# Two units side by side between the chunks of x, and own buffers for the third unit

## Chip, cores, metric

One core of one Trainium2 chip. The metric is the device time of one execution in microseconds (us).

## What is computed

One decoder layer over 16 learned tokens and 512 prompt positions, and for 8 decode sequences with a cache: 536 tokens in all, 1024 channels, in this order:

```python
x = x + 0.5 * (silu(h @ w_gate1) * (h @ w_up1)) @ w_down1     # h = rmsnorm(x)
u, q, k, v = project(rmsnorm(x))                              # QK-norm, partial rotary
x = x + concat(pool_mix(u), window_attention(q, k, v)) @ w_out
x = x + 0.5 * (silu(h @ w_gate2) * (h @ w_up2)) @ w_down2     # h = rmsnorm(x)
```

The inner width of both feed-forward halves is 2816, that is 22 blocks of 128. All of it is float32.

## The kernel before

Everything lies transposed: channels on the 128 partitions, tokens along the rows. x is 8 chunks (`xT[:, k, :]`, 128 channels x 536 tokens, 268 KB). Each operand of a large product is split in two: a high part, rounded to the type that TensorE takes in one pass (`xhi`, `whi`), and the rest (`xlo`, `wlo`). A product is then three: high by high, weights' high by x's low, weights' low by x's high. ScalarE makes the high parts, VectorE the low ones, and semaphores count what is done. A matmul takes 268 tokens, so each of the three comes as two matmuls.

The first half of the layer begins with "plain" units, the change's place. A unit is one block of 128 columns of gate or up weights: 8 tiles of 128x128, 512 KB, 48 matmuls. Units 0 and 1 are gate and up of the first block, 2 and 3 of the second, and so on up to unit 7; unit c is loaded into `raw[:, c % 3]` and split into `whi[:, c % 2]` and `wlo[:, c % 2]` (`whi_of`, `wlo_of`, lines 420 to 424). Behind them, from line 740 on, stand larger blocks that use a scheme with fewer products; their weights' high parts are in `whi7`.

The order on each engine is written out by hand:

- SyncE (lines 521 to 531) loads the first two tiles of unit 0 (`FIRST`), two chunks of x, the other six tiles, six chunks of x, then units 1 and up. x comes in `ORDER` 0, 2, 4, 6, 1, 3, 5, 7. A load into a slot of `raw` that is taken again waits for the low part that was made from it (line 477).
- ScalarE (lines 1306 to 1330) makes the high parts in that order, then the split of unit 1, the squares of x (`sqx`) with the split of unit 2 behind the fourth, the even chunks scaled (`x_even`), a table load for the root, the split of unit 3, the root of the norm, and the first sums of the later scheme (`t_hi`). From unit 2 on a split waits for the unit before the last one, whose buffer it takes (line 1117).
- VectorE (lines 1765 to 1797) makes the low parts, scales two small tables, makes the low part of unit 1, adds the squares up one after the other with the low part of unit 2 behind the fourth sum, then four terms of `t_sums`, the low part of unit 3, and the reciprocal of the root (`invert`).
- TensorE (lines 693 to 708) runs `WARM` products of zeros, then `early`: unit 0's high parts chunk by chunk, its products with x's low parts, unit 1 in the same manner. Unit 2 stands in three pieces with the norm between them:

```python
plain(2, turn, [0, 1])
norm_sums(0, 0, n)          # waits for all seven sums of squares
plain(2, turn, [2, 3])
norm_spread(0, 0, n, 1)     # waits for the reciprocal
plain(2, turn, [4, 5, 6, 7])
```

Then come unit 3 (it waits for the spread norm) and units 4 to 7.

Of the kernel before, what the change touches and what calls it, by code (L numbers as in the profile page):

```python
# [39 lines left out]
P = 128  # L40
# [69 lines left out]

NORM_AT = (1, 2, 6)
SQSUM_AT = (0, KD - 1, 2 * (KD - 1))
WARM = 6
FIRST = 2
ORDER = (0, 2, 4, 6, 1, 3, 5, 7)


# [31 lines left out]
def build(nc, a):  # L149
# [90 lines left out]
    dq, o = place("dq", [P, NDEC, KVH, GQ], offset=o)  # L240
    assert o <= h_at

    o = whi7_at
    ckT, o = place("ckT", [P, NDEC, P], offset=o)
    cv, o = place("cv", [P, NDEC, P], offset=o)
# [46 lines left out]
    def sem(name):  # L292
        return ctx.enter_context(nc.semaphore(name))
# [1 line left out]
    x_loaded = [sem(f"x_loaded{k}") for k in range(KD)]  # L295
    fixed_loaded = sem("fixed_loaded")
    gains_loaded = sem("gains_loaded")
    first_loaded = sem("first_loaded")
    first_hi = sem("first_hi")
    first_lo = sem("first_lo")  # L300
    mixin_loaded = sem("mixin_loaded")
# [116 lines left out]
              dict(s=1, ua=U_A2, ub=U_B2, ea=E_A2, eb=E_B2, c0=META, n=NH_OUT)]  # L418

    def whi_of(c):  # L420
        return whi3 if c == U_OUT + 2 else whi[:, c % 2, :, :]

    def wlo_of(c):
        return wlo3 if c == U_OUT + 2 else wlo[:, c % 2, :, :]

    def blocks(n):

# [45 lines left out]
    def _(sp):  # L473
# [40 lines left out]
        def downs(s, p):  # L514

            for d in range(KD):
                load_down(s, p, d)
                if d == 3 and p < 2:
                    load_unit(s, p + 1, 0)

        sp.dma_start(raw[:, 0, 0:FIRST, :].rearrange("p t c -> p (t c)"), a["gu1"][:, 0:FIRST * P]
                     ).then_inc(first_loaded, 16)
        for k in ORDER:
            sp.dma_start(xT[:, k, :], a["x"][:, k, :]).then_inc(x_loaded[k], 16)
            if k == ORDER[FIRST - 1]:
                sp.dma_start(raw[:, 0, FIRST:KD, :].rearrange("p t c -> p (t c)"), a["gu1"][:, FIRST * P:KD * P]
                             ).then_inc(raw_loaded[0], 16)
        for u in range(1, 2 * PLAIN[0]):
            load_plain(0, u)
            if u == 5:  # L530
                load_unit(0, 0, 0)
# [68 lines left out]
    def _(pe):  # L600
# [31 lines left out]
            for _ in range(WARM):  # L632
                nc.tensor.matmul(nsum[:, 0, 0:2 * P], hid[:, 0:P], hid[:, 0:2 * P], start=True, stop=True)

        def early(c, dst, pairs, n, wait, first=False, last=False):

            x = x_split(n)
            for t, k in enumerate(ORDER):
                for i, (w, lo) in enumerate(pairs):
                    wait(t, i)  # L640
                    for h in range(2):
                        done = nc.tensor.matmul(dst[:, h, 0:n], w[:, c % 2, t, :], x(k, lo, h),  # L642
                                                start=(first and t == 0 and i == 0),
                                                stop=(last and t == KD - 1 and i == len(pairs) - 1))
            if last:
                done.then_inc(unit_done, 1)

        def norm_sums(i, c0, n):

# [17 lines left out]
        def plain_products_1():  # L667

            n = NH_ALL

            def hi_there(t, i):
                if i == 0:
                    pe.wait_ge(xhi_ready, t + 1)
                if t == 0:
                    pe.wait_ge(first_lo if i else first_hi, 1)
                elif t == FIRST:
                    pe.wait_ge(wlo_ready if i else whi_ready, 1)

            def lo_there(t, i):
                pe.wait_ge(xlo_ready, t + 1)  # L680

            def hi_1(t, i):
                if t + i == 0:
                    pe.wait_ge(whi_ready, 2)

            def lo_1(t, i):
                if t == 0:
                    pe.wait_ge(wlo_ready, 2)

            def plain(c, dst, ks=None):  # L690
                product(c, dst, KD, x_split(n), n, None, ks, chunk)

            warm_up()
            early(0, pair[0], [(whi, 0), (wlo, 0)], n, hi_there, first=True)
            early(0, pair[0], [(whi, 1)], n, lo_there, last=True)
            early(1, pair[1], [(whi, 0), (whi, 1)], n, hi_1, first=True)
            early(1, pair[1], [(wlo, 0)], n, lo_1, last=True)
            plain(2, turn, [0, 1])
            norm_sums(0, 0, n)
            plain(2, turn, [2, 3])  # L700
            norm_spread(0, 0, n, 1)
            plain(2, turn, [4, 5, 6, 7])
            pe.wait_ge(rstd_ready, 1)
            plain(3, nsum)
            for f in (2, 3):
                for j in range(2):
                    pe.wait_ge(evacuated, E_A1 + 2 * f + j - (3 if f == 2 else 1))
                    plain(2 * f + j, pair[j])
# [391 lines left out]
    def _(act):  # L1100
# [7 lines left out]
        def split_hi(c):  # L1108

            t = tiles_of(c)  # L1110
            act.wait_ge(raw_loaded[c % RAW], 16 * (c // RAW + 1))
            if c == U_OUT + 2:
                act.wait_ge(sin_ready, 5)
                act.wait_ge(rot_ready, 5)
                act.wait_ge(nsum_filled, 5)
            elif c >= 2:
                act.wait_ge(unit_done, c - 1)
            nc.scalar.copy(whi_of(c)[:, 0:t, :], raw[:, c % RAW, 0:t, :]).then_inc(whi_ready, 1)  # L1118

# [185 lines left out]

        act.wait_ge(consts_made, 2)
        nc.scalar.copy(warm[:, :], eps[:, :]).then_inc(warmed, 1)
        act.wait_ge(first_loaded, 16)
        nc.scalar.copy(whi[:, 0, 0:FIRST, :], raw[:, 0, 0:FIRST, :]).then_inc(first_hi, 1)
        act.wait_ge(gains_loaded, 16)  # L1310
        for k in ORDER:
            act.wait_ge(x_loaded[k], 16)
            x_hi(x_pair(xhi7, k, NH_ALL), k, 0, 0, NH_ALL)
            if k == ORDER[FIRST - 1]:
                act.wait_ge(raw_loaded[0], 16)
                nc.scalar.copy(whi[:, 0, FIRST:KD, :], raw[:, 0, FIRST:KD, :]).then_inc(whi_ready, 1)
        split_hi(1)
        for k in range(KD):
            nc.scalar.activation(sqx[:, k, :], xT[:, k, :], ACT.Square).then_inc(sqx_ready, 1)
            if k == 3:  # L1320
                split_hi(2)
        late_consts()
        for pr in range(KC):
# [178 lines left out]
    def _(dve):  # L1502
# [259 lines left out]
                    if d:  # L1762
                        add_square(1, d, 0, NH_ALL)

        def first_weights_lo(hi_there, tiles):

            dve.wait_ge(hi_there, 1)
            return nc.vector.tensor_tensor(wlo[:, 0, tiles, :], raw[:, 0, tiles, :], whi[:, 0, tiles, :].bitcast(F32),
                                           ALU.subtract)

        first_weights_lo(first_hi, slice(0, FIRST)).then_inc(first_lo, 1)
        dve.wait_ge(gains_loaded, 16)
        for t, k in enumerate(ORDER):
            x_lo(x_pair(xlo7, k, NH_ALL), x_pair(xhi7, k, NH_ALL), t, k, 0, 0, NH_ALL)
            if t == FIRST - 1:
                first_weights_lo(whi_ready, slice(FIRST, KD)).then_inc(wlo_ready, 1)
        dve.wait_ge(fixed_loaded, 16)
        nc.vector.tensor_scalar(nsink[:, :], fixed[:, C_SINK:C_IDENT], -1.0, None, ALU.mult)
        nc.vector.tensor_scalar(ngain[:, :], gains[:, 0:3 * KD], -1.0, None, ALU.mult).then_inc(ngain_made, 1)
        split_lo(1)  # L1780

        for k in range(1, KD):
            dve.wait_ge(sqx_ready, k + 1)
            if k > 1:
                dve.wait_ge(sqx_summed, k - 1)
            nc.vector.tensor_tensor(sqx[:, 0, :], sqx[:, 0, :], sqx[:, k, :], ALU.add).then_inc(sqx_summed, 1)
            if k == 4:
                split_lo(2)
        dve.wait_ge(ngain_made, 1)
        n = NH_ALL  # L1790
# [434 lines left out]
```

## Time and profile before

| | us |
|---|---|
| median of the runs | 882.77 (881.46 to 883.40, 3 runs) |
| profiled execution, its time | 880.45 |
| profiled execution, its span | 878.4 |
| TensorE busy in the span | 871.3 (99%) |
| VectorE, ScalarE, GpSimd busy | 660.3, 394.0, 32.4 |

Times in the rows are from the start of the span. A row names line, engine, operation, what is written and read, and a count; matmuls overlap, so that the length of a group is from the first start to the last end.

### The profile page before, as it was taken

The numbers are of one execution on the slowest core, as the hardware profiler recorded it, in microseconds if no ns is written. First come the engines' busy times: TensorE is split into PE (matmuls) and PEld (weight loads), VectorE is DVE, ScalarE is ACT, GpSimd is POOL, SyncE is SP. The second block draws the span as 40 slices with busy tenths as digits, with TensorE's granted clock in tenths as the row PEclk, the third lists the DMA queues.
The fourth block names the chain that finished last, engine by engine and source line by source line (L and its number), as shares of the span: only waits on it lengthen the run. The fifth ranks groups of instructions, "written<-read, shape, count | busy, mean of one in ns | idle before, by whom it ended". The sixth has DMA issues, their size and how long they took to land.

```text
span 878.4 us, 17072 instructions
## 1 busy us (share of the span) xinstructions
PE 871.3 (99%) x7088; PEld 856.9 (98%) x7088; DVE 660.3 (75%) x979; ACT 394.0 (45%) x639; POOL 32.4 (4%) x37
## 2 busy tenths in 40 slices
PE   8999999999999999999999999999999999999998
PEld 7999999999999999999888999999999999999998
DVE  6979647997569986754887697996479975799754
ACT  7635313554224553443754465554125542255420
POOL 0000000000000000012423000000000000000000
PEclk9999999999999999999999999999999999999999
DMA  7333323332424322522321415324233324334241
GB/s 251 117 121 114 133 66 121 121 121 84 145 65 164 121 76 84 190 76 60 113 65 60 145 38 169 120 76 175 75 121 120 121 85 145 111 122 128 85 121 61
DMA packets 43180, 98.57 MB, mean 112 GB/s; under 512 B 4288, under 2 KB 5056, under 8 KB 43104
## 3 DMA queue, kind: packets, MB, share of 16 engines
q1 hardware_dynamic: 41376, 95.01, 33.6%
q10 hardware_dynamic: 1728, 2.48, 0.8%
q8 instruction: 56, 0.92, 0.4%
q14 instruction: 20, 0.16, 0.1%
HBM read 93.53 MB, written 3.60 MB: 111 GB/s over the span
## 4 chain that ended last, share of the span: by engine, by line
PE 96%; DVE 2%; DMA 1%; issue 1%; ACT 0%; SPq 0%; DVEq 0%; ACTq 0%
PE ps L612 44%; PE ps L740 15%; PE ps L742 15%; PE ps L741 15%; PE ps L642 1%; PE ps L978 1%; PE ps L969 1%; DMA xT<-x 1%; PE ps L960 1%; PE ps L799 1%; PE ps L933 0%; PE ps L883 0%; PE ps L657 0%; DVE wlo L1522 0%; DVE hlo L1649 0%
## 5 line engine op out<-in xcount | busy, mean ns | idle before, releaser
L740 PE MATMUL ps<-xhi,whi 128*128 128x260 f32 (+1 forms) x1092 | 310.2, 284 | 0.1
L742 PE MATMUL ps<-xhi,wlo 128*128 128x260 f32 (+1 forms) x1092 | 310.0, 284 | 0.0
L741 PE MATMUL ps<-xlo,whi 128*128 128x260 f32 (+1 forms) x1092 | 309.6, 284 | 0.0
L740 PEld LDWEIGHTS ps<-xhi,whi 128*128 128x128 f32 x1092 | 205.4, 188 | 0.8 <-issue 0.6
L742 PEld LDWEIGHTS ps<-xhi,wlo 128*128 128x128 f32 x1092 | 205.5, 188 | 0.0
L741 PEld LDWEIGHTS ps<-xlo,whi 128*128 128x128 f32 x1092 | 205.4, 188 | 0.0
L1593 DVE TENSOR_TENSOR wlo<-full,whi 128x1024 fp32r<-128x1024 f32 (+1 forms) x117 | 160.3, 1394 | 0.0
L1118 ACT CAST whi<-raw 128x1024 fp32r<-128x1024 f32 (+1 forms) x75 | 75.2, 1003 | 154.9 <-PE ps L612 147.9
L612 PE MATMUL ps<-hhi,whi 128*128 128x268 f32 (+1 forms) x690 | 140.4, 285 | 0.3
L612 PE MATMUL ps<-hlo,whi 128*128 128x268 f32 (+1 forms) x690 | 140.1, 284 | 0.0
L612 PE MATMUL ps<-hhi,wlo 128*128 128x268 f32 (+1 forms) x690 | 139.8, 284 | 0.0
L612 PEld LDWEIGHTS ps<-hhi,whi 128*128 128x128 f32 x690 | 106.8, 188 | 1.1 <-DVE hlo L1649 1.1
L612 PEld LDWEIGHTS ps<-hhi,wlo 128*128 128x128 f32 x690 | 107.0, 188 | 0.0
L612 PEld LDWEIGHTS ps<-hlo,whi 128*128 128x128 f32 x690 | 106.7, 188 | 0.0
L1522 DVE TENSOR_TENSOR wlo<-raw,whi 128x1024 fp32r<-128x1024 f32 (+1 forms) x75 | 90.2, 1204 | 16.9 <-ACT whi L1118 16.8
L1689 DVE SCALAR_TENSOR_TENSOR gate<-ps,rstd 128x536 f32<-128x536 f32 (+1 forms) x47 | 33.2, 707 | 81.6 <-PE ps L612 81.2
L1178 ACT CAST whi<-full 128x1024 fp32r<-128x1024 f32 x39 | 41.1, 1053 | 106.4 <-issue 89.6
L612 PE MATMUL ps<-xhi,whi 128*128 128x268 f32 (+1 forms) x288 | 60.5, 291 | 0.0
L612 PE MATMUL ps<-xhi,wlo 128*128 128x268 f32 (+1 forms) x288 | 58.7, 285 | 0.0
L612 PE MATMUL ps<-xlo,whi 128*128 128x268 f32 (+1 forms) x288 | 58.5, 285 | 0.0
L1192 ACT CAST whi<-full 128x1536 fp32r<-128x1536 f32 x39 | 57.8, 1483 | 0.0
L1578 DVE TENSOR_TENSOR full<-full 128x1024 f32<-128x1024 f32 x39 | 47.4, 1216 | 0.0
(194 smaller groups left out, 1070.4 us busy)
## 6 DMA issues: line engine op xcount, KB each, us to landing
full<-gu SPq DMA_DIRECT2D x78, 512.0 KB, 4.4
raw<-d SPq DMA_DIRECT2D x32, 448.0 KB, 3.5
full<-gu SPq DMA_DIRECT2D x39, 256.0 KB, 2.7
raw<-d SPq DMA_DIRECT2D x16, 512.0 KB, 3.7
raw<-w_in SPq DMA_DIRECT2D x10, 512.0 KB, 3.7
raw<-gu SPq DMA_DIRECT2D x9, 512.0 KB, 4.3
raw<-w_out SPq DMA_DIRECT2D x8, 512.0 KB, 4.3
xT<-x SPq DMA_DIRECT2D x8, 268.0 KB, 5.8
```

Source lines behind the costliest of these rows:

```text
L612: last = nc.tensor.matmul(dst[:, h, 0:n], w[:, kk, :], x(k, lo, h), start=(k == begin and i == 0), stop=(k == end and i == 2))
L642: done = nc.tensor.matmul(dst[:, h, 0:n], w[:, c % 2, t, :], x(k, lo, h), start=(first and t == 0 and i == 0), stop=(last and t == KD - 1 ...
L740: nc.tensor.matmul(dst, whi_t, xhi_t, start=(first and pr == 0), stop=False, skip_group_check=True)
L741: nc.tensor.matmul(dst, whi_t, xlo_t, start=False, stop=False, skip_group_check=True)
L742: last = nc.tensor.matmul(dst, wlo_t, xhi_t, start=False, stop=(pr == KC - 1), skip_group_check=True)
L1118: nc.scalar.copy(whi_of(c)[:, 0:t, :], raw[:, c % RAW, 0:t, :]).then_inc(whi_ready, 1)
L1178: nc.scalar.copy(whi7[:, i % 2, 0:2, :], full[:, i % 3, 0:2, :]).then_inc(hi_ready[0], 1)
L1192: nc.scalar.copy(whi7[:, i % 2, 4:7, :], full[:, i % 3, 4:7, :]).then_inc(hi_ready[2], 1)
L1522: nc.vector.tensor_tensor(wlo_of(c)[:, 0:t, :], raw[:, c % RAW, 0:t, :], whi_of(c)[:, 0:t, :].bitcast(F32), ALU.subtract).then_inc(wlo_rea ...
L1578: nc.vector.tensor_tensor(full[:, r, 1:5:3, :], full[:, r, 1:5:3, :], full[:, r, 0:7:6, :], ALU.add).then_inc(added, 1)
L1593: nc.vector.tensor_tensor(wlo7[:, i % 3, b, :], full[:, i % 3, b, :], whi7[:, i % 2, b, :].bitcast(F32), ALU.subtract).then_inc(lo_ready[g ...
L1689: nc.vector.scalar_tensor_tensor(out=halves(gate[:, cols], n), in0=pair[d % 2][:, :, 0:n], scalar=-0.5, in1=halves(rstd[:, cols], n), op0= ...
```

## The change

The loads of units 0 and 1 are cut into three pieces each (two, two and four tiles) and stand between the chunks of x: ahead of the first chunk unit 0's first piece, ahead of the second unit 1's first, ahead of the third both second pieces, ahead of the fifth both last ones. ScalarE and VectorE split each piece in the same place of their order. TensorE takes the two units side by side: for each chunk of x the products with its high part for both units, then those with the low part of the chunk before. Both units end together. One warm-up product is dropped. The split of unit 2 goes to buffers of its own (`whi_u2`, `wlo_u2`, in the second half of `whi7`, which is free until the later scheme's second block), doesn't wait for unit 0, and moves from behind the fourth square to behind the second; its low part moves from behind the fourth sum to behind the first.

```diff
--- before.py
+++ after.py
@@ -110,8 +110,10 @@
 
 NORM_AT = (1, 2, 6)
 SQSUM_AT = (0, KD - 1, 2 * (KD - 1))
-WARM = 6
-FIRST = 2
+WARM = 5
+PIECES = ((0, 2), (2, 4), (4, 8))
+
+BEFORE_X = {0: ((0, 0),), 1: ((1, 0),), 2: ((0, 1), (1, 1)), 4: ((0, 2), (1, 2))}
 ORDER = (0, 2, 4, 6, 1, 3, 5, 7)
 
 
@@ -240,6 +242,9 @@
     dq, o = place("dq", [P, NDEC, KVH, GQ], offset=o)
     assert o <= h_at
 
+    whi_u2, o = place("whi_u2", [P, KD, P], F32R, offset=whi7_at + 7 * BLK * 4)
+    wlo_u2, o = place("wlo_u2", [P, KD, P], F32R, offset=o)
+    assert o <= w_end
     o = whi7_at
     ckT, o = place("ckT", [P, NDEC, P], offset=o)
     cv, o = place("cv", [P, NDEC, P], offset=o)
@@ -295,7 +300,7 @@
     x_loaded = [sem(f"x_loaded{k}") for k in range(KD)]
     fixed_loaded = sem("fixed_loaded")
     gains_loaded = sem("gains_loaded")
-    first_loaded = sem("first_loaded")
+    piece_loaded = [[sem(f"piece_loaded{c}{j}") for j in range(2)] for c in range(2)]
     first_hi = sem("first_hi")
     first_lo = sem("first_lo")
     mixin_loaded = sem("mixin_loaded")
@@ -418,10 +423,10 @@
               dict(s=1, ua=U_A2, ub=U_B2, ea=E_A2, eb=E_B2, c0=META, n=NH_OUT)]
 
     def whi_of(c):
-        return whi3 if c == U_OUT + 2 else whi[:, c % 2, :, :]
+        return {2: whi_u2, U_OUT + 2: whi3}.get(c, whi[:, c % 2, :, :])
 
     def wlo_of(c):
-        return wlo3 if c == U_OUT + 2 else wlo[:, c % 2, :, :]
+        return {2: wlo_u2, U_OUT + 2: wlo3}.get(c, wlo[:, c % 2, :, :])
 
     def blocks(n):
 
@@ -518,14 +523,16 @@
                 if d == 3 and p < 2:
                     load_unit(s, p + 1, 0)
 
-        sp.dma_start(raw[:, 0, 0:FIRST, :].rearrange("p t c -> p (t c)"), a["gu1"][:, 0:FIRST * P]
-                     ).then_inc(first_loaded, 16)
-        for k in ORDER:
+        def load_piece(c, j):
+            lo, hi = PIECES[j]
+            sp.dma_start(raw[:, c, lo:hi, :].rearrange("p t c -> p (t c)"), a["gu1"][:, (c * KD + lo) * P:(c * KD + hi) * P]
+                         ).then_inc(raw_loaded[c] if j == 2 else piece_loaded[c][j], 16)
+
+        for t, k in enumerate(ORDER):
+            for c, j in BEFORE_X.get(t, ()):
+                load_piece(c, j)
             sp.dma_start(xT[:, k, :], a["x"][:, k, :]).then_inc(x_loaded[k], 16)
-            if k == ORDER[FIRST - 1]:
-                sp.dma_start(raw[:, 0, FIRST:KD, :].rearrange("p t c -> p (t c)"), a["gu1"][:, FIRST * P:KD * P]
-                             ).then_inc(raw_loaded[0], 16)
-        for u in range(1, 2 * PLAIN[0]):
+        for u in range(2, 2 * PLAIN[0]):
             load_plain(0, u)
             if u == 5:
                 load_unit(0, 0, 0)
@@ -632,18 +639,31 @@
             for _ in range(WARM):
                 nc.tensor.matmul(nsum[:, 0, 0:2 * P], hid[:, 0:P], hid[:, 0:2 * P], start=True, stop=True)
 
-        def early(c, dst, pairs, n, wait, first=False, last=False):
+        def first_two(n):
 
             x = x_split(n)
-            for t, k in enumerate(ORDER):
-                for i, (w, lo) in enumerate(pairs):
-                    wait(t, i)
-                    for h in range(2):
-                        done = nc.tensor.matmul(dst[:, h, 0:n], w[:, c % 2, t, :], x(k, lo, h),
-                                                start=(first and t == 0 and i == 0),
-                                                stop=(last and t == KD - 1 and i == len(pairs) - 1))
-            if last:
-                done.then_inc(unit_done, 1)
+            for t in range(KD + 1):
+                for c in range(2):
+                    if t == KD:
+                        break
+                    if c == 0:
+                        pe.wait_ge(xhi_ready, t + 1)
+                    for i, w in enumerate((whi, wlo)):
+                        if t in (0, 2):
+                            pe.wait_ge(first_lo if i else first_hi, t + c + 1)
+                        elif t == 4:
+                            pe.wait_ge(wlo_ready if i else whi_ready, c + 1)
+                        for h in range(2):
+                            nc.tensor.matmul(pair[c][:, h, 0:n], w[:, c, t, :], x(ORDER[t], 0, h),
+                                             start=(t == 0 and i == 0), stop=False)
+                if t:
+                    pe.wait_ge(xlo_ready, t)
+                    for c in range(2):
+                        for h in range(2):
+                            done = nc.tensor.matmul(pair[c][:, h, 0:n], whi[:, c, t - 1, :], x(ORDER[t - 1], 1, h),
+                                                    start=False, stop=(t == KD))
+                        if t == KD:
+                            done.then_inc(unit_done, 1)
 
         def norm_sums(i, c0, n):
 
@@ -668,33 +688,11 @@
 
             n = NH_ALL
 
-            def hi_there(t, i):
-                if i == 0:
-                    pe.wait_ge(xhi_ready, t + 1)
-                if t == 0:
-                    pe.wait_ge(first_lo if i else first_hi, 1)
-                elif t == FIRST:
-                    pe.wait_ge(wlo_ready if i else whi_ready, 1)
-
-            def lo_there(t, i):
-                pe.wait_ge(xlo_ready, t + 1)
-
-            def hi_1(t, i):
-                if t + i == 0:
-                    pe.wait_ge(whi_ready, 2)
-
-            def lo_1(t, i):
-                if t == 0:
-                    pe.wait_ge(wlo_ready, 2)
-
             def plain(c, dst, ks=None):
                 product(c, dst, KD, x_split(n), n, None, ks, chunk)
 
             warm_up()
-            early(0, pair[0], [(whi, 0), (wlo, 0)], n, hi_there, first=True)
-            early(0, pair[0], [(whi, 1)], n, lo_there, last=True)
-            early(1, pair[1], [(whi, 0), (whi, 1)], n, hi_1, first=True)
-            early(1, pair[1], [(wlo, 0)], n, lo_1, last=True)
+            first_two(n)
             plain(2, turn, [0, 1])
             norm_sums(0, 0, n)
             plain(2, turn, [2, 3])
@@ -1113,7 +1111,7 @@
                 act.wait_ge(sin_ready, 5)
                 act.wait_ge(rot_ready, 5)
                 act.wait_ge(nsum_filled, 5)
-            elif c >= 2:
+            elif c > 2:
                 act.wait_ge(unit_done, c - 1)
             nc.scalar.copy(whi_of(c)[:, 0:t, :], raw[:, c % RAW, 0:t, :]).then_inc(whi_ready, 1)
 
@@ -1305,19 +1303,23 @@
 
         act.wait_ge(consts_made, 2)
         nc.scalar.copy(warm[:, :], eps[:, :]).then_inc(warmed, 1)
-        act.wait_ge(first_loaded, 16)
-        nc.scalar.copy(whi[:, 0, 0:FIRST, :], raw[:, 0, 0:FIRST, :]).then_inc(first_hi, 1)
-        act.wait_ge(gains_loaded, 16)
-        for k in ORDER:
+
+        def piece_hi(c, j):
+
+            lo, hi = PIECES[j]
+            act.wait_ge(raw_loaded[c] if j == 2 else piece_loaded[c][j], 16)
+            nc.scalar.copy(whi[:, c, lo:hi, :], raw[:, c, lo:hi, :]).then_inc(whi_ready if j == 2 else first_hi, 1)
+
+        for t, k in enumerate(ORDER):
+            for c, j in BEFORE_X.get(t, ()):
+                piece_hi(c, j)
+            if t == 0:
+                act.wait_ge(gains_loaded, 16)
             act.wait_ge(x_loaded[k], 16)
             x_hi(x_pair(xhi7, k, NH_ALL), k, 0, 0, NH_ALL)
-            if k == ORDER[FIRST - 1]:
-                act.wait_ge(raw_loaded[0], 16)
-                nc.scalar.copy(whi[:, 0, FIRST:KD, :], raw[:, 0, FIRST:KD, :]).then_inc(whi_ready, 1)
-        split_hi(1)
         for k in range(KD):
             nc.scalar.activation(sqx[:, k, :], xT[:, k, :], ACT.Square).then_inc(sqx_ready, 1)
-            if k == 3:
+            if k == 1:
                 split_hi(2)
         late_consts()
         for pr in range(KC):
@@ -1762,29 +1764,29 @@
                     if d:
                         add_square(1, d, 0, NH_ALL)
 
-        def first_weights_lo(hi_there, tiles):
-
-            dve.wait_ge(hi_there, 1)
-            return nc.vector.tensor_tensor(wlo[:, 0, tiles, :], raw[:, 0, tiles, :], whi[:, 0, tiles, :].bitcast(F32),
-                                           ALU.subtract)
-
-        first_weights_lo(first_hi, slice(0, FIRST)).then_inc(first_lo, 1)
-        dve.wait_ge(gains_loaded, 16)
+        def piece_lo(c, j):
+
+            lo, hi = PIECES[j]
+            dve.wait_ge(whi_ready if j == 2 else first_hi, c + 1 if j == 2 else 2 * j + c + 1)
+            nc.vector.tensor_tensor(wlo[:, c, lo:hi, :], raw[:, c, lo:hi, :], whi[:, c, lo:hi, :].bitcast(F32),
+                                    ALU.subtract).then_inc(wlo_ready if j == 2 else first_lo, 1)
+
         for t, k in enumerate(ORDER):
+            for c, j in BEFORE_X.get(t, ()):
+                piece_lo(c, j)
+            if t == 0:
+                dve.wait_ge(gains_loaded, 16)
             x_lo(x_pair(xlo7, k, NH_ALL), x_pair(xhi7, k, NH_ALL), t, k, 0, 0, NH_ALL)
-            if t == FIRST - 1:
-                first_weights_lo(whi_ready, slice(FIRST, KD)).then_inc(wlo_ready, 1)
         dve.wait_ge(fixed_loaded, 16)
         nc.vector.tensor_scalar(nsink[:, :], fixed[:, C_SINK:C_IDENT], -1.0, None, ALU.mult)
         nc.vector.tensor_scalar(ngain[:, :], gains[:, 0:3 * KD], -1.0, None, ALU.mult).then_inc(ngain_made, 1)
-        split_lo(1)
 
         for k in range(1, KD):
             dve.wait_ge(sqx_ready, k + 1)
             if k > 1:
                 dve.wait_ge(sqx_summed, k - 1)
             nc.vector.tensor_tensor(sqx[:, 0, :], sqx[:, 0, :], sqx[:, k, :], ALU.add).then_inc(sqx_summed, 1)
-            if k == 4:
+            if k == 1:
                 split_lo(2)
         dve.wait_ge(ngain_made, 1)
         n = NH_ALL
```

## Rows read from the trace of the kernel before

**Rows 1.** The page, busy us, share of the span and instructions.
```profile
PE 871.3 (99%) x7088; PEld 856.9 (98%) x7088; DVE 660.3 (75%) x979; ACT 394.0 (45%) x639; POOL 32.4 (4%) x37
```
**Rows 2.** Stretches: busy PE, PEld, DVE, ACT, POOL (instructions), granted clock, DMA share, GB/s.
```profile
1.20:6.10 4.90, 4.90 (x12) 3.91 (x13) 1.00 (x6) 3.09 (x5) 0.00 (x0) 1.00 0.89 264
6.10:7.60 1.50, 1.47 (x10) 1.20 (x8) 1.02 (x2) 0.84 (x2) 0.00 (x0) 1.00 0.94 326
7.60:8.80 1.20, 0.00 (x0) 0.00 (x0) 0.96 (x1) 0.83 (x3) 0.00 (x0) 1.00 1.02 347
8.80:12.75 3.95, 3.93 (x24) 3.20 (x25) 3.95 (x6) 3.47 (x6) 0.00 (x0) 1.00 1.04 417
```
**Rows 3.** Timeline of TensorE to 9 us: start, length, what, idle before.
```profile
1.18 5.40 PE L633 MATMUL ps<-hid 128*128 128x256 f32 x12 [1.18 <-DVE hid L1511]
...
6.11 0.72 PE L642 MATMUL ps<-xhi,whi 128*128 128x268 f32 x2
...
8.82 0.52 PE L642 MATMUL ps<-xhi,whi 128*128 128x268 f32 x2 [1.25 <-ACT xhi L1128]
```
**Rows 4.** Timeline of TensorE from 12 to 26 us.
```profile
12.87 2.14 PE L642 MATMUL ps<-xlo,whi 128*128 128x268 f32 x16
...
20.77 0.41 PE L612 MATMUL ps<-xhi,whi 128*128 128x268 f32 x2
...
22.25 1.17 PE L657 MATMUL ps<-ones,sqx 128*128 128x1 f32 x10
...
24.86 0.71 PE L664 MATMUL ps<-fixed,nrm 128*128 128x128 f32 x5
```
**Rows 5.** Timeline of ScalarE in the head.
```profile
4.79 1.38 ACT L1128 ACTIVATE xhi<-xT,fixed 128x536 fp32r<-128x536 f32 x2 [1.34 <-DMA xT<-x]
...
8.03 4.19 ACT L1128 ACTIVATE xhi<-xT,fixed 128x536 fp32r<-128x536 f32 x6 [0.37 <-DMA xT<-x]
12.70 1.05 ACT L1118 CAST whi<-raw 128x1024 fp32r<-128x1024 f32 x1 [0.48 <-DMA raw<-gu]
13.65 1.73 ACT L1319 ACTIVATE sqx<-xT 128x536 f32<-128x536 f32 x3
...
18.94 1.74 ACT L1132 ACTIVATE t<-xT,fixed 128x268 f32<-128x268 f32 x4
...
22.10 1.03 ACT L1118 CAST whi<-raw 128x1024 fp32r<-128x1024 f32 x1
```
**Rows 6.** Timeline of VectorE in the head.
```profile
8.80 4.26 DVE L1528 SCALAR_TENSOR_TENSOR xlo<-xT,fixed,xhi 128x536 fp32r<-128x536 f32 x6 [0.16 <-ACT xhi L1128]
...
13.05 0.17 DVE L1779 TENSOR_SCALAR ngain<-fixed 128x24 f32<-128x24 f32 x1
13.78 1.23 DVE L1522 TENSOR_TENSOR wlo<-raw,whi 128x1024 fp32r<-128x1024 f32 x1 [0.56 <-ACT whi L1118]
14.92 2.35 DVE L1786 TENSOR_TENSOR sqx<-sqx 128x536 f32<-128x536 f32 x3
...
18.08 1.22 DVE L1522 TENSOR_TENSOR wlo<-raw,whi 128x1024 fp32r<-128x1024 f32 x1
19.21 2.36 DVE L1786 TENSOR_TENSOR sqx<-sqx 128x536 f32<-128x536 f32 x3
...
23.25 1.22 DVE L1522 TENSOR_TENSOR wlo<-raw,whi 128x1024 fp32r<-128x1024 f32 x1
24.38 0.18 DVE L1678 RECIPROCAL nrm<-nrm 128x5 f32<-128x5 f32 x1
```
**Rows 7.** Timeline of SyncE's DMA issues, the last six chunks of x.
```profile
2.58 3.29 SPq L524 DMA_DIRECT2D xT<-x  x6
```
**Rows 8.** Timeline of TensorE at 446 us, and stretches near 425 us (columns as rows 2).
```profile
446.06 1.14 PE L933 MATMUL ps<-gate,poolw 128*128 128x260 f32 x4
...
423.50:425.40 1.90, 1.17 (x12) 0.49 (x8) 1.79 (x8) 1.90 (x4) 1.28 (x1) 1.00 0.05 9
425.40:427.40 2.00, 2.00 (x20) 1.77 (x16) 1.08 (x5) 1.72 (x7) 0.00 (x0) 1.00 0.14 25
```

## Prediction

> **What bounds the kernel now.** I read the page first: TensorE is busy 99% of the span [rows 1], so a change can only pay where TensorE waits, and the diff touches only the first 25 us. I then cut that head into stretches [rows 2] and read the timeline of TensorE in them [rows 3, 4]. There is one visible hole: matmuls start at 6.11, the first four pairs are through at 7.57, and the next starts at 8.82 after 1.25 us of idle put down to the high part of the third chunk of x [rows 3]. From 8.82 TensorE is fed more thinly than it could be until 12.87, and from there on it is packed: 16 matmuls in 2.14 us, less the tail of about 0.29 of the last one, is 0.123 us each [rows 4]. Unit 2 begins at 20.77. Units 0 and 1 are 96 matmuls, 96 x 0.123 = 11.8 us; between 6.11 and 20.77 there are 14.66 us. So some 2.8 us of waiting lie in the head, and that is the most this reordering can win there.
>
> The second thing to read is what runs beside it. The sums of squares on VectorE end at 19.21 + 2.36 = 21.57, and TensorE comes to its norm sums (L657) at 22.25 [rows 4, 6]: 0.6 us of slack. The reciprocal is done at 24.38 + 0.18 = 24.56, and TensorE comes to the spreading (L664) at 24.86 [rows 4, 6]: 0.3 us. These two chains are nearly as late as TensorE itself. That decides the forecast.
>
> **The change, part by part.**
>
> *Units 0 and 1 side by side.* The same 96 matmuls run in another order. Each chunk of x now feeds 12 of them instead of 4 until unit 0 is through, so TensorE is less often starved. It starts at about 5.6, not 6.11: one warm-up less frees 5.40/6 = 0.9 us [rows 3], and the first high part of x begins at 4.79 [rows 5] and takes about 0.75. It waits at 6.2 for the low part of unit 1's first piece (VectorE, about 6.8), and once more for the high part of the third chunk, which lands as late as before, since the same bytes stand ahead of it: about 8.9. From there 76 matmuls are left (6 chunks x 8 high ones, 7 x 4 low ones): 76 x 0.123 = 9.4, end 18.3. The last chunk doesn't bind: 16 matmuls after its high part (about 13.7, below) end at 15.7. So units 0 and 1 end at about 18.3, and unit 2 starts 2.4 us earlier. With its first two chunks (12 matmuls, 1.5 us) TensorE stands at the norm sums at 19.8 instead of 22.25.
>
> *The transfers.* All of x and units 0 and 1 are 8 x 268 + 1024 KB in both kernels. Before, unit 1 came last of these and its cast started at 12.70, released by the DMA, while the last chunk's high part was already done at 8.03 + 4.19 = 12.22 [rows 5], so that chunk had landed at about 11.5. Now unit 1's pieces stand ahead of the last chunks, so the last chunk lands when unit 1 did: 12.7, or 1.2 us later. The three transfers more, and shorter rows, add an unknown e. Bounds: if the thin rate of 6.1 to 8.8 (326 to 347 GB/s) came from the order before and goes up to the 417 of the next stretch [rows 2], 2.7 x (1 - 336/417) = 0.5 us is gained; if 326 lasted through the 3.95 us at 417, 3.95 x (417/326 - 1) = 1.1 us is lost. I take e = +0.2: chunks of x landed at 268 KB per 0.70 us (six high parts in 4.19 us), unit 1's 512 KB in 1.2 us after the last of them, so rows as short as x's cost 512 KB about 0.1 us more, and the pieces' rows are shorter still. SyncE's issues don't bind: six take 3.29 us [rows 7], so the 14th begins at 0.74 + 13 x 0.55 = 7.9 at the latest, 5 us ahead of its landing.
>
> The Trainium skill (DMA: Bandwidth & Descriptors, "Anatomy of one DMA" and "Bandwidth") puts a fixed cost of some 2 us on each DMA, fitted on the GpSimd path, and advises large ones, which speaks against this split; taken in series, three more would be an estimated 6 us, some 888 in all. The trace doesn't agree for queued transfers: chunks landed 0.70 us apart.
>
> *ScalarE and VectorE behind x.* Last chunk lands 12.9; its high part ends at 12.9 + 0.75 = 13.65. VectorE's low part ends 0.84 later (before 12.22 to 13.06 [rows 5, 6]): 14.5; the two small scalings until 14.65. ScalarE's squares follow directly, since the split of unit 1 (1.05 us, 12.70) is gone from here: the first begins at 13.55, and with 0.55 from start to start and 0.64 for one (three in 1.73) the second ends at 14.75, then the split of unit 2 runs from 14.65 to 15.7. On VectorE the low part of unit 1 (1.23) is gone too. First sum 14.8 to 15.55, then a wait of 0.2 for the split, low part of unit 2 15.75 to 16.95 (1.22), six sums. One sum to the next is 0.82 (three in 2.36, the last 0.72): end 16.87 + 5 x 0.82 + 0.72 = 21.7. Before it was 21.57. The later x takes 1.2 + 0.2, the two splits moved away and the idle time beside them give back 1.3.
>
> *What is late next.* TensorE, ready for the norm sums at 19.8, waits until 21.8: about 2 us of the 2.4 won stand there. It leaves them 0.45 earlier than before, does 12 matmuls and comes to the spreading at 24.4. From the last sum to the reciprocal VectorE is packed: four terms, the low part of unit 3 (23.25, 1.22), the reciprocal; 24.56 - 21.57 = 3.0 us. Reciprocal at 24.7, spreading at 24.8, against 24.86. **So 0.1 us of the 2.4 arrives**; the rest is a wait on VectorE's chain. ScalarE doesn't come later than that: the split of unit 3 stands 3.2 us behind the start of the even chunks [rows 5] and moves with the squares, by -0.1 to +0.1.
>
> *Buffers for unit 2.* Its split no longer waits for unit 0, which now ends with unit 1 at 18.3; without them the split would stand at 18.3 rather than 14.65 and push the sums by over 2 us. So they cost nothing and save what the pairing would else lose. Unit 3's split waits for unit 1 (18.3) and has its place on ScalarE at about 22: nothing. On SyncE the load of unit 3 waits for unit 0's low part (now about 11 instead of 8.65) behind a queue that is full until unit 2 has landed (about 14): nothing. Later loads go earlier. After the spreading TensorE is packed, so the shift goes to the end unchanged.
>
> **The sum.** Profiled execution 880.45 (span 878.4 and 2.05 around it) - 0.1 = 880.35. With e from -0.5 to +1.1 the shift is -0.7 to +0.8. The profiled execution is 2.32 under the median of the runs, 882.77, so the forecast for the median is **882.7**, and 882.0 to 883.6 for this case.
>
> **The rivals.**
> *The gain gets through.* If the sums of squares aren't the bound (VectorE's chain 2 us shorter than I reckon), all 2.4 us arrive: 882.77 - 2.4 = 880.4. For it: nobody waits for them now. Against: every term is a row, and they are on VectorE one after the other.
> *Pieces slow the transfers (slower).* If the whole 3.95 us ran at the 264 GB/s of the first stretch [rows 2], 3.95 x (417/264 - 1) = 2.3 us later x, and with VectorE as the bound 2.0 us of it arrive: 884.8. It begins to cost from e = 0.3 on. Against: that stretch has the start-up of the queue in it. The fixed cost that the Trainium skill's DMA page states, taken in series, would be the same mechanism at a higher price.
> *The clock falls (slower).* The new wait of 2 us, followed by matmuls of one column, is longer than the 1.25 us of before. The warm-up ran 12 passes of 256 columns in 5.40 us, 0.45 each, against 4 passes of 260 in 1.14, 0.29, later on [rows 3, 8]: the lower level of 1.2 GHz, though the view prints 1.00 there. To come up again at that rate for 5.4 us would lose about 2.7: 885.4. Against: the stretch at 425.4 with 20 small matmuls, and the 1.9 us before it with TensorE busy for 1.17, kept 1.00 [rows 8]. The Trainium skill (TensorE: Matmul & The Clock Gate, "HAM oscillation") warns that waits between bursts of matmuls throttle TensorE; the trace shows no fall at its holes.
> *It doesn't pair.* If pieces come so late that TensorE starves as before, units 0 and 1 end up to 2 us later than 18.3: still ahead of the sums, the same 882.7.
>
> **How the numbers follow.** Forecast, with the case that it doesn't pair: 0.80. Gain gets through: 0.12. Transfers: 0.04. Clock: 0.04. A measurement of this kernel tells 0.2% (1.8 us) from no change, and the runs of before spread over 1.9. The range takes the forecast's case with about 1 us of scatter and reaches down to the gain: 880.5 to 884.3. Faster 0.12, same 0.80, slower 0.08.
>
> **What would show it.** Right: in the profile after, unit 2's first matmul near 18.3; a wait of about 2 us ahead of L657's matmuls put down to the sums of squares; the sums ending near 21.7; L664's matmuls near 24.8; a packed TensorE behind. Wrong: sums that end before 20 (faster), a last high part of x later than 15, or a granted clock under 1.00 behind 20 us (slower).

## The result and the profile after

The changed kernel takes 883.73 us, the kernel before 881.82 us, each the median of 21 runs made side by side. The ratio is 1.0018 with a 95% interval of 1.0011 to 1.0025: slower by about 1.6 us by the ratio and 1.9 by the medians, where no change that a measurement can tell (-0.1 us) was forecast.

| | before | after |
|---|---|---|
| median of 21 runs, us | 881.82 | 883.73 |
| profiled execution, its time, us | 880.45 | 882.80 |
| its span, us | 878.4 | 880.9 |
| its mean granted clock | 1.000 | 0.998 |

The granted clock is TensorE's clock as a share of its full level; the two levels in these traces are 1.00 and 0.50 ("half clock"), and a stretch at 0.50 is called a fall below.

The timeline of TensorE in the head of the changed kernel (start, length, what, idle before), which answers to rows 3 and 4:

```profile
8.78 0.52 PE L657 MATMUL ps<-xhi,whi 128*128 128x268 f32 x2 [0.24 <-ACT xhi L1126]
...
12.66 0.52 PE L657 MATMUL ps<-xhi,whi 128*128 128x268 f32 x2 [0.49 <-ACT xhi L1126]
...
18.18 1.15 PE L663 MATMUL ps<-xlo,whi 128*128 128x268 f32 x8
19.16 0.41 PE L619 MATMUL ps<-xhi,whi_u 128*128 128x268 f32 x2
...
22.70 1.28 PE L677 MATMUL ps<-ones,sqx 128*128 128x1 f32 x10 [1.90 <-DVE sqx L1788]
...
25.70 0.76 PE L684 MATMUL ps<-fixed,nrm 128*128 128x128 f32 x5
```

Unit 2 starts at 19.16 instead of 20.77, so the pairing works. Then TensorE waits 1.90 us for the sums of squares, where it did not wait before, and the spreading comes at 25.70 against 24.86 [rows 4]: all of the gain and 0.84 us more are gone. VectorE and ScalarE in the same execution, beside rows 5 and 6:

```profile
12.64 2.84 DVE L1530 SCALAR_TENSOR_TENSOR xlo<-xT,fixed,xhi 128x536 fp32r<-128x536 f32 x4
...
16.70 1.23 DVE L1524 TENSOR_TENSOR wlo_u<-raw,whi_u 128x1024 fp32r<-128x1024 f32 x1 [0.22 <-ACT whi_u L1116]
17.84 4.81 DVE L1788 TENSOR_TENSOR sqx<-sqx 128x536 f32<-128x536 f32 x6
...
25.46 0.18 DVE L1680 RECIPROCAL nrm<-nrm 128x5 f32<-128x5 f32 x1
...
11.86 2.77 ACT L1126 ACTIVATE xhi<-xT,fixed 128x536 fp32r<-128x536 f32 x4
14.54 1.18 ACT L1321 ACTIVATE sqx<-xT 128x536 f32<-128x536 f32 x2
```

The chain is the one that was reckoned, link by link, but about 1 us later: the last high part of x ends at 14.63, not at 13.65, and the sums at 22.65, not at 21.7. The stretches (columns as in rows 2) tell where that came from:

```profile
6.10:7.60 1.50, 1.38 (x11) 1.17 (x10) 1.37 (x4) 1.09 (x3) 0.00 (x0) 1.00 0.90 265
7.60:8.80 1.20, 0.96 (x9) 0.74 (x7) 0.51 (x3) 0.74 (x1) 0.00 (x0) 1.00 0.92 262
8.80:12.75 3.95, 3.46 (x25) 3.17 (x25) 2.92 (x5) 2.76 (x5) 0.00 (x0) 1.00 0.98 356
```

The transfers ran at 265, 262 and 356 GB/s, against 326, 347 and 417 [rows 2]. In this execution they were slow; the runs below show that they mostly are not. And much later, in the attention stage, the clock was at half for about 5.40 x (1 - 0.68)/0.5 = 3.5 us, which it was not in the profiled execution of the kernel before (after, then before):

```profile
428.60:434.00 5.40, 5.40 (x35) 5.38 (x32) 2.39 (x3) 2.18 (x6) 2.63 (x3) 0.68 0.68 202
...
428.60:434.00 5.40, 5.36 (x44) 4.22 (x43) 3.95 (x10) 3.25 (x5) 4.69 (x5) 1.00 0.73 241
```

So one profile beside one profile shows two things at once, 0.9 us in the head (the first matmul of the later scheme at 58.93 for 58.05) and 1.5 us from there to the end, and neither need be what separates the medians. Each run has a mean granted clock, and sorting the runs by it separates the two. Times are means; in brackets is the number of runs. The runs of before are the 29 that were made beside the first four experiments; of the 21 beside the changed kernel only the times were kept, and the highest of them, 883.78, is close to the highest of the 29, 883.55.

| mean granted clock | before | after |
|---|---|---|
| 0.999 to 1.000 | 880.1 (6) | none |
| 0.997 to 0.998 | 881.8 (15) | 882.25 (5) |
| 0.996 | 883.2 (8) | 883.4 (8) |
| 0.994 | none | 884.7 (8) |

At equal clock the changed kernel is only 0.2 to 0.5 us over the kernel before. But its executions lie lower in the table. Half the clock for 3.5 us is 1.7 us of 880, or 0.002 of the mean: a step in the table, and it costs 1.1 to 1.7 us. On average the changed kernel has one such step more than the kernel before (2.1 against 1.1). The question was therefore where these falls are, and whether the change makes them.

### The profile page after: what moved, and what is told of

The parts are those of the page before. It is cut to its first block, busy times and chain, and to the rows that moved or that the text cites. A ratio compares the mean times of both kernels' runs of the same rounds, so it can differ in the third digit from the quotient of the medians.

```text
span 880.9 us, 17077 instructions
## 1 busy us (share of the span) xinstructions
PE 872.2 (99%) x7086; PEld 857.7 (97%) x7086; DVE 660.8 (75%) x982; ACT 394.4 (45%) x642; POOL 32.4 (4%) x37
## 4 chain that ended last, share of the span: by engine, by line
PE 94%; DVE 3%; ACT 1%; DMA 1%; issue 1%; SPq 1%; DVEq 0%; ACTq 0%
PE ps L619 44%; PE ps L738 15%; PE ps L740 15%; PE ps L739 15%; PE ps L976 1%; PE ps L967 1%; DMA xT<-x 1%; PE ps L958 1%; PE ps L797 1%; PE ps L931 0%; DVE wlo L1524 0%; DVE sqx L1788 0%; PE ps L881 0%; DVE hlo L1651 0%; DVE hid L1644 0%
## 5 line engine op out<-in xcount | busy, mean ns | idle before, releaser
L1116 ACT CAST whi<-raw 128x1024 fp32r<-128x1024 f32 (+1 forms) x73 | 73.1, 1001 | 154.3 <-PE ps L619 147.8
L1524 DVE TENSOR_TENSOR wlo<-raw,whi 128x1024 fp32r<-128x1024 f32 (+1 forms) x73 | 87.8, 1204 | 16.3 <-ACT whi L1116 16.0
L619 PE MATMUL ps<-xhi,whi 128*128 128x268 f32 (+1 forms) x272 | 57.7, 294 | 0.0
L619 PE MATMUL ps<-xlo,whi 128*128 128x268 f32 (+1 forms) x272 | 55.9, 287 | 0.0
L619 PE MATMUL ps<-xhi,wlo 128*128 128x268 f32 (+1 forms) x272 | 55.9, 287 | 0.0
```

The lines of the kernel that those rows point to most:

```text
L619: last = nc.tensor.matmul(dst[:, h, 0:n], w[:, kk, :], x(k, lo, h), start=(k == begin and i == 0), stop=(k == end and i == 2))
L1524: nc.vector.tensor_tensor(wlo_of(c)[:, 0:t, :], raw[:, c % RAW, 0:t, :], whi_of(c)[:, 0:t, :].bitcast(F32), ALU.subtract).then_inc(wlo_rea ...
```

## The experiments

Theory A: the wait at the norm sums, which the prediction foresaw, lets the clock fall in some of the executions, and that is most of the loss. Theory B: the falls lie in the attention stage alone and have to do with the time at which that stage comes. Theory C: the order of the transfers, the buffers or the move of the split cost the time by themselves. All runs of a group were made on one chip beside runs of the kernel before. The first group (the filled wait, everything later, the norm later, the load order) stands beside 881.85, the second (the first further execution, the same move without the pairing, the two on buffers) beside 881.73. The other four further executions were made on another chip, beside a single run of before (880.05).

**The wait, filled.**

```diff
-        def warm_up():
+        def warm_up(count=WARM):
...
-            for _ in range(WARM):
+            for _ in range(count):
...
             plain(2, turn, [0, 1])
+            warm_up(4)
             norm_sums(0, 0, n)
```

> The changed kernel with four products of zeros (8 passes, about 1.7 us) in the wait ahead of the norm sums; nothing else waits for them, and they end before the sums of squares do. Theory A (falls of the clock behind that wait cost part of the loss): fewer falls in a run, 0.5 to 1 us faster than the changed kernel, about 882.9, with the head as late as there (spreading at 25.7). Theory B (falls elsewhere): the time of the changed kernel, 883.7, and its mean granted clocks of 0.994 to 0.998.

Measured: 882.05 us, ratio to the kernel before 1.0003 (0.9994 to 1.0013). The changed kernel's loss is gone, more of it than either theory had. Of 11 runs one is at 0.999, seven at 0.998 (mean 881.97), three at 0.996, none at 0.994: the kernel before's clocks. In its profile the products of zeros end where the sums arrive, and the stretch behind them is at full clock:

```profile
19.97 1.89 PE L640 MATMUL ps<-hid 128*128 128x256 f32 x8
21.70 1.23 PE L677 MATMUL ps<-ones,sqx 128*128 128x1 f32 x10
...
24.65 0.76 PE L684 MATMUL ps<-fixed,nrm 128*128 128x128 f32 x5
...
22.50:29.40 6.90, 6.78 (x55) 6.56 (x56) 6.28 (x11) 4.38 (x7) 0.00 (x0) 1.00 0.35 114
```

Work that nobody needs made the kernel 1.7 us faster than the changed one (by the medians; each stands beside its own runs of the kernel before, 881.85 and 881.82). It lets nothing end earlier; all that it does is to keep TensorE busy. One more thing is to be read here: the spreading is at 24.65, not at 25.70. In this execution x landed about as reckoned, so the expected lateness in the head was that of one execution.

**The changed kernel again, five executions for their clock.** No edit. What the expectations call a look is one such execution; here they are executions 1 (on the chip of the other experiments) and 2 to 5.

> The changed kernel once more, for its clock. Theory A (the wait at the norm sums lets the clock fall): a stretch of a few us at half clock that begins between 20 and 27 us, beside one or none in the attention stage (420 to 460 us). Theory B: falls in the attention stage alone. With x landing as in the last profiles (12.8), the sums end at about 21.6 and the spreading comes at about 24.7.

> The changed kernel again, one of four equal looks at its clock. Theory A (the wait at the norm sums lets the clock fall, in some of the executions): where the mean granted clock is 0.996 or lower, a stretch at half clock that begins between 20 and 27 us stands in the profile. Theory B: all falls lie in the attention stage (420 to 460 us), in every one of the four.

Executions 3, 4 and 5 had the expectation of execution 2. Measured, in order: 882.11, 881.74, 883.29, 881.76 and 883.12 us; mean granted clocks 0.998, 0.998, 0.996, 0.998, 0.996. The two at 0.996 have the fall in the head, and none in the attention stage. The three at 0.998 have one in the attention stage and none in the head. Executions 3 and 4, the same kernel, from 22.5 us on and in the attention stage:

```profile
22.50:29.40 6.90, 6.90 (x33) 6.90 (x33) 6.04 (x12) 3.58 (x7) 0.00 (x0) 0.51 0.39 124
...
420.00:460.00 40.00, 39.14 (x310) 32.78 (x308) 35.35 (x110) 27.55 (x80) 14.23 (x13) 1.00 0.30 97
```

```profile
22.50:29.40 6.90, 6.77 (x55) 6.55 (x56) 6.51 (x12) 4.39 (x7) 0.00 (x0) 1.00 0.43 134
...
420.00:460.00 40.00, 39.14 (x297) 32.78 (x296) 33.66 (x103) 26.85 (x76) 12.94 (x12) 0.96 0.28 85
```

Granted clock 0.51 against 1.00, 33 matmuls against 55 in the same 6.9 us. The timeline of execution 3 shows the fall behind the wait, and what it does to a pair of matmuls: 0.65 us in place of 0.41.

```profile
21.81 1.62 PE L677 MATMUL ps<-ones,sqx 128*128 128x1 f32 x10 [1.90 <-DVE sqx L1788]
23.29 0.79 PE L619 MATMUL ps<-xhi,whi_u 128*128 128x268 f32 x2
23.89 0.65 PE L619 MATMUL ps<-xlo,whi_u 128*128 128x268 f32 x2
...
26.12 1.27 PE L684 MATMUL ps<-fixed,nrm 128*128 128x128 f32 x5
...
29.67 0.41 PE L619 MATMUL ps<-xhi,whi_u 128*128 128x268 f32 x2
```

The price is read at the first matmul of the later scheme, where the head is over. In the kernel before, in execution 4 and in execution 3, in this order:

```profile
58.05 0.28 PE L740 MATMUL ps<-xhi,whi 128*128 128x268 f32 x1
```

```profile
58.11 0.28 PE L738 MATMUL ps<-xhi,whi 128*128 128x268 f32 x1
```

```profile
60.83 0.28 PE L738 MATMUL ps<-xhi,whi 128*128 128x268 f32 x1
```

Without a fall in the head the changed kernel stands there at 57.74 (execution 2), 58.08 (execution 1) and 58.11, beside 58.05 before; the forecast for it was 57.95 (58.05 less 0.1). With one it stands at 60.83 and 60.60 (execution 5): 2.7 us later. The wait itself was 1.46 to 1.90 us in all five; whether the clock falls behind it differs from execution to execution. Both falls stand behind a wait of 1.90 us, which two profiles without a fall have too (execution 4 and the first profile); what decides is not shown.

A fall in the head counts two steps of the table, since the executions that have it and no other are at 0.996. The kernel before reaches 0.996 in another way: the profile of "buffers and the moved split alone" below is at 0.996 too, with two falls in the attention stage and none in the head. No execution at 0.994 was profiled, so that it is a fall in the head beside one in the attention stage is concluded from the sizes. For it speaks where such clocks occur: 0.995 or less stands in 8 of the 26 runs of the changed kernel, 3 of 6 and 4 of 4 of the two experiments below whose profiles show a fall in the head, and in none of the 103 runs of the other kernels whose clock is on record.

**Everything later by 0.9 us, without a new wait** (the kernel before, changed behind unit 7):

```diff
                     plain(2 * f + j, pair[j])
+            for _ in range(4):
+                nc.tensor.matmul(nsum[:, 0, 0:P], ident[:, :], ident[:, :], start=True, stop=True)
```

> The kernel before with four transposes of the identity (about 0.9 us of TensorE) behind unit 7, so that everything from there on is late by as much as in the changed kernel and nothing else is changed. If the falls of the clock in a run depend on where the attention stage lies in time: about 1.9 us over the kernel before, as the changed kernel. If they don't: 0.9 us over it, 882.7.

Measured: 882.80 us, ratio 1.0017 (1.0006 to 1.0027), that is 0.95 us over the kernel before by the medians, with its clocks (six of 11 runs at 0.998, three at 0.996, none below). The interval, 0.5 to 2.4 us, doesn't tell 0.9 from 1.9; the clocks do, and at equal clock the delayed kernel is 0.8 us (0.998) and 1.1 us (0.996) over the kernel before. Theory B falls: a later attention stage doesn't bring more falls.

**The norm later in unit 2.**

```diff
-            plain(2, turn, [0, 1])
+            plain(2, turn, [0, 1, 2, 3])
             norm_sums(0, 0, n)
-            plain(2, turn, [2, 3])
+            plain(2, turn, [4, 5])
             norm_spread(0, 0, n, 1)
-            plain(2, turn, [4, 5, 6, 7])
+            plain(2, turn, [6, 7])
```

> The changed kernel with two more chunks of unit 2 (12 matmuls, 1.5 us) ahead of the norm sums, and the spreading behind the sixth chunk. Theory A (the changed kernel loses 0.85 us at the spreading since x lands late, and the rest to falls of the clock behind the 1.9 us wait at the norm sums): the wait shrinks to about 0.5 us, the spreading comes at about 25.7 with 12 matmuls more behind it, so 1.5 us are won and the extra falls go: about 881.2, 0.6 under the kernel before, with a mean granted clock per run higher than that of the changed kernel. Theory B (the extra falls have nothing to do with that wait): only the 1.5 us are won, about 882.2.

Measured: 880.35 us, ratio 0.9985 (0.9975 to 0.9996): faster than both kernels, 1.5 us under the one before and 3.4 under the changed one, and 0.85 under the 881.2 of theory A, which had x landing as late as in the first profile. Two of 12 runs are at full clock, none is at 0.994. The wait is down to 0.39 us:

```profile
21.68 1.28 PE L677 MATMUL ps<-ones,sqx 128*128 128x1 f32 x10 [0.39 <-DVE sqx L1788]
24.67 0.76 PE L684 MATMUL ps<-fixed,nrm 128*128 128x128 f32 x5
...
56.43 0.28 PE L738 MATMUL ps<-xhi,whi 128*128 128x268 f32 x1
```

The sums and the spreading come no earlier than in the filled kernel, but 12 matmuls of work (12 x 0.123 = 1.5 us) have moved ahead of them.

**The same move without the pairing** (the diff above on the kernel before).

> The kernel before with the norm sums behind the fourth chunk of unit 2 and the spreading behind the sixth, nothing else. TensorE didn't wait for the sums there, so if the 1.5 us of norm_later are the gain of the units side by side, let through: nothing moves, 881.8. If the place of the norm alone is what pays: 880.4, as norm_later.

Measured: 881.92 us, ratio 1.0002 (0.9988 to 1.0015). Nothing: the place of the norm is worth something only once TensorE comes to it early. The 1.5 us are the gain of the change, let through.

**Load order without the pairing** (the changed kernel, with TensorE's order of units 0 and 1 from the kernel before):

```diff
...
             warm_up()
-            first_two(n)
+            early(0, pair[0], [(whi, 0), (wlo, 0)], n, hi_there, first=True)
+            early(0, pair[0], [(whi, 1)], n, lo_there, last=True)
+            early(1, pair[1], [(whi, 0), (whi, 1)], n, hi_1, first=True)
+            early(1, pair[1], [(wlo, 0)], n, lo_1, last=True)
```

> The changed kernel's loads, splits and buffers, but TensorE takes unit 0 and then unit 1 as before. If the order of the transfers makes x late and that is what costs: the last low part of x at about 15.5, unit 0 done at about 17, unit 1 at 22.8, spreading at about 26.9, 2.1 us later than in the kernel before: about 883.9, and no long wait at the norm sums. If the load order is free and taking the units side by side is what costs: the time of the kernel before, 881.8.

Measured: 884.41 us, ratio 1.0038 (1.0023 to 1.0053), 2.6 us over the kernel before where 2.1 were expected, but not for the reason given alone. At equal clock it is 1.2 us (two runs at 0.996) and 1.4 us (one at 0.998) over runs of before. The rest is the clock again: in the profiled execution TensorE, fed by unit 0 alone, waits for chunks (the wait is the row's last field) and is at half clock from 10.4 on.

```profile
11.24 0.82 PE L675 MATMUL ps<-xhi,whi 128*128 128x268 f32 x2 [1.53 <-ACT xhi L1161]
...
10.40:17.30 6.90, 6.06 (x27) 6.07 (x28) 6.35 (x11) 6.86 (x12) 0.00 (x0) 0.51 0.82 326
```

So the load order (with one warm-up product fewer) has a price when nothing is paired with it, and the pairing pays it.

**Buffers and the moved split alone** (the kernel before with `whi_u2`, `wlo_u2`, and the split and low part of unit 2 in the new places).

```diff
-            if k == 3:
+            if k == 1:
                 split_hi(2)
...
-            if k == 4:
+            if k == 1:
                 split_lo(2)
```

> The kernel before with the buffers of unit 2 and the split of unit 2 in its new places on ScalarE and VectorE, nothing else. By rows of the kernel before the sums end at about 21.8 instead of 21.57, TensorE has 0.6 us of slack there and the spreading stays at 24.9: 881.8. If the buffers or the move are what costs: 0.4 to 2 us over it.

Measured: 881.70 us, ratio 0.9994 (0.9981 to 1.0008). This part is free, as expected.

**The changed kernel without the buffers.**

```diff
-        return {2: whi_u2, U_OUT + 2: whi3}.get(c, whi[:, c % 2, :, :])
+        return whi3 if c == U_OUT + 2 else whi[:, c % 2, :, :]
...
-            elif c > 2:
+            elif c >= 2:
                 act.wait_ge(unit_done, c - 1)
```

> The changed kernel with unit 2 split into the buffer of unit 0, so that its split waits for unit 0 (done at about 18.3 with unit 1). By the prediction's step the split comes 3.7 us later, the sums end at about 25.3 and the reciprocal at 28.3: spreading 3.5 us later than in the kernel before, with two waits of TensorE of 2 to 3 us and falls of the clock behind them: 886.5 to 888. If the buffers don't matter: 883.7, as the changed kernel.

Measured: 888.35 us, ratio 1.0072 (1.0053 to 1.0092). That is a little more than expected: without the buffers the change costs 6.6 us, not 1.9. In the profiled execution TensorE waited 2.2 us for unit 2's low part, until 20.66, and 1.96 us for the sums, and the clock was at half for 10.3 us, from behind the first wait on:

```profile
25.39 2.29 PE L677 MATMUL ps<-ones,sqx 128*128 128x1 f32 x10 [1.96 <-DVE sqx L1788]
...
21.00:31.30 10.30, 8.34 (x40) 8.02 (x38) 9.27 (x17) 6.67 (x12) 0.00 (x0) 0.50 0.69 228
```

Theory C falls for the buffers and the moved split. For the transfers a small part stays: 0.2 to 0.5 us at equal clock.

## Why the prediction was wrong

**The chain in the head was right.** Unit 2 starts 1.6 us earlier in the profiled execution, TensorE stands 1.9 us at the norm sums, VectorE's chain is the bound, and almost nothing of the gain arrives. Where the clock held in the head, it was over at 57.74 to 58.11, for a forecast of 57.95; only the first profiled execution was later, at 58.93, since its transfers were slow. The wait that the forecast put in the place of the old one measured 1.46 to 1.90 us for 2.

**The step that failed** is the price of the new wait: in the sum it costs nothing but its own length, and the clock behind it stands only in the rival "the clock falls", with a chance of 0.04. Its mechanism, its place and its price, 2.7 us, were in the prediction, and 2.7 us is what a fall in the head cost. Two of six profiles of the changed kernel have it, and eight of its 21 runs are at 0.994, where the kernel before has none. On average it has one step of 1.1 to 1.7 us more (a fall in the head in about half of the runs, as an estimate, since one is two steps), and that with the 0.2 to 0.5 us at equal clock covers the 1.6 to 1.9 between the kernels.

**What was luck.** The price agrees by two misses: the clock was at half for 6.90 x (1 - 0.51)/0.5 = 6.8 us, not for the 5.4 of the prediction, and 1 us at half clock cost 2.7/6.8 = 0.4 us, not 0.5. And 883.73 is only 1.0 us from the forecast of 882.7 because the three runs of before that it started from had their median 0.95 us over that of the 21.

**Why the chance was too small.** The argument against it was that the clock stayed at 1.00 in thin stretches near 425 us [rows 8]. That was true of one execution. Of the 29 runs of the kernel before only three are at exactly 1.000 and three at 0.999. The changed kernel's execution 4 shows 0.96 over the attention stage, and the stage's code is the same in both kernels. So these rows, read in several executions, would have spoken for the rival: with TensorE busy for the same 1.17 us between 423.5 and 425.4, the granted clock from 428 to 430 is 0.50 in the profile of the same move without the pairing and in that of the buffers alone, which have the head of the kernel before with small edits, and 1.00 in its own. So a granted clock under 1.00 anywhere behind 20 us, which was to be the sign of the rival, tells nothing by itself; one between 20 and 30 us does. The Trainium skill (TensorE: Matmul & The Clock Gate, "HAM oscillation") warns that waits between bursts of matmuls throttle TensorE. The two falls behind waits of 1.90 us bear it out, against the single trace.

**The estimate e.** Taken as +0.2 us, it was +1.2 in the first profiled execution (the last high part ended at 14.63 where 13.45 would be e = 0) and -0.2 to +0.4 in the nine others with this load order (13.21 to 13.82). The upper bound of 1.1 was just too low for one execution; for the others the value was good. At the lower bound of -0.5 the shift is -0.8 us, not the -0.7 that the prediction has.

**The other steps** held: the buffers cost nothing and save much (without them 4.6 us over the changed kernel, where "over 2 us" was put, clock and all), and the rival that the gain gets through describes the kernel with the later norm, where 1.5 of the 2.4 us arrive. What the dropped warm-up product does by itself was not tried: the first pairs behind the warm-up took 0.65 to 0.82 us in execution 2, which still had the earliest end of the head.

**What stays open.** The changed kernel had many runs only in the first comparison. Its five later executions have a median of 882.11 and none at 0.994; they are too few to tell whether the fall in the head comes as often there as in the 21 runs, and the filled kernel and the one with the later norm were not run beside the changed one.

## What to carry to other kernels

A gain that ends in a wait is not always worth zero: if TensorE is the engine that waits, a fall of the clock behind the wait can make it worth less than zero, here in some executions only, so that one profile can't rule it out. Read the granted clock of several runs before a thin stretch is called safe. And when an engine is fed earlier, move the work that depends on the next-slowest chain back by as much: here two lines, `norm_sums` and `norm_spread`, turned 1.9 us lost into 1.5 us won.

## What was not expected of the hardware

Dummy matmuls on zeros in a wait of 1.9 us bought 1.7 us of median time, though no result came earlier. Where the clock falls differs between executions of the same code: five of one kernel gave two with 2.7 us lost in the head and three with 1.2 to 1.6 us lost in the attention stage (from the first matmul of the later scheme to the end they took 823.7 to 824.0 us, the other two 822.5). And the same transfers into the head ended, by the high part of the last chunk of x, 0.8 to 1.4 us later in one execution than in the nine others.
